# Modulation of mixer 0 loaded in four pieces of columns, gate sums moved into the products and chunks

## What is computed

```python
mod = (silu(c) @ ada_w + ada_b)                       # 6 * 1024 columns
sh1, sc1, g1, sh2, sc2, g2 = split(mod, 6)
h = rmsnorm(x, norm1_g) * (1 + sc1) + sh1
x = x + g1 * hybrid_mixer(h, ...)                     # w_in, conv, SSD chunks, gMLP, w_out
h = rmsnorm(x, norm2_g) * (1 + sc2) + sh2
x = x + g2 * conv_gated_ffn(h, ...)
out = rmsnorm(x, final_g)
```

## Time and profile before

| | |
|---|---|
| median of 3 runs | 2769.61 us (2765.91 to 2772.1) |
| profiled execution, its own time | 2763.87 us |
| its span | 2762.1 us |
| TensorE busy in the span | 2697.5 us |
| VectorE, ScalarE, GpSimd busy | 1815.1, 1003.4, 1072.4 us |
| granted TensorE clock, mean of the span | 0.994 |

### The profile page before, as it was taken

The page is one execution under the profiler, slowest core; times in us unless marked ns, Lnnn a source line. Parts: engine busy times, 40 slices in busy tenths (PEclk is TensorE's granted clock), DMA queues, the critical chain, the costliest instruction groups (busy, mean ns, idle before and its releaser), DMA issues.

```text
span 2762.1 us, 33801 instructions
## 1 busy us (share of the span) xinstructions
PE 2697.5 (98%) x12427; PEld 2207.2 (80%) x12427; DVE 1815.1 (66%) x2544; ACT 1003.4 (36%) x1521; POOL 1072.4 (39%) x739
## 2 busy tenths in 40 slices
PE   7999999999999999999999999999999999999998
PEld 6777887787878888887878888888888788887886
DVE  6977956768287565568787565555746855455767
ACT  3543325321153333343535322152223433334333
POOL 3444435445057777654650100001102544444240
PEclk9999999999999999999999999999999999999999
DMA  9876877999846566483448767587676334445646
GB/s 383 281 268 246 313 263 248 349 328 315 287 129 218 201 207 217 157 293 96 148 160 298 236 211 280 177 284 235 210 261 201 117 116 127 126 125 207 217 167 221
DMA packets 261872, 616.29 MB, mean 223 GB/s; under 512 B 26597, under 2 KB 84425, under 8 KB 257611
## 3 DMA queue, kind: packets, MB, share of 16 engines
q1 hardware_dynamic: 261046, 613.89, 64.9%
q10 hardware_dynamic: 662, 0.24, 0.0%
HBM read 462.37 MB, written 151.66 MB: 222 GB/s over the span
## 4 chain that ended last, share of the span: by engine, by line
PE 82%; DVE 6%; DMA 5%; issue 3%; POOL 2%; SPq 1%; ACT 1%; DVEq 0%; ACTq 0%; POOLq 0%
PE main L2038 34%; PE pair L2310 15%; PE main L2310 14%; PE pair L2330 6%; PE main L2330 5%; DMA w_split_scratch<-w_hl 2%; PE pair L2179 2%; POOL w_hl L739 1%; PE pair L2204 1%; PE pair L2164 1%; PE pair L2171 1%; DVE a_lo L1659 1%; DMA ada_t<-in_ada_w_dram 1%; DMA w_hl<-w_split_scratch 1%; POOL tb L750 1%
## 5 line engine op out<-in xcount | busy, mean ns | idle before, releaser
L739 POOL TENSOR_TENSOR w_hl<-w_raw,w_hl 128x512 fp32r<-128x512 f32 x548 | 794.2, 1455 | 920.5 <-ACT w_hl L844 918.8
L844 ACT ACTIVATE w_hl<-w_raw 128x512 fp32r<-128x512 f32 x548 | 342.3, 630 | 831.9 <-PE main L2310 169.4
L2038 PE MATMUL main<-w_hl,h_hi 128*128 128x512 f32 x1536 | 493.4, 403 | 5.1 <-DMA w_hl<-w_split_scratch 2.8
L2038 PEld LDWEIGHTS main<-w_hl,h_hi 128*128 128x128 f32 x1536 | 285.9, 189 | 77.8 <-issue 14.7
L2038 PE MATMUL main<-w_hl,h_lo 128*128 128x512 f32 x768 | 301.3, 392 | 0.0
L781 POOL TENSOR_TENSOR pre_hl<-pre_raw,pre_hl 128x512 fp32r<-128x512 f32 x35 | 51.0, 1461 | 566.3 <-ACT pre_hl L868 566.3
L2038 PE MATMUL main<-h_hi,w_hl 128*128 128x512 f32 x768 | 247.7, 396 | 7.4 <-POOL w_hl L739 4.2
L750 POOL TENSOR_TENSOR tb<-tb,tb 128x512 f32<-128x512 f32 x132 | 198.1, 1501 | 113.9 <-DMA tb<-in_ff_up_dram 109.5
L2310 PE MATMUL pair<-s_hi,w_hl 128*128 128x512 f32 x736 | 235.8, 393 | 2.4 <-POOL w_hl L739 2.4
L2330 PE MATMUL main<-w_hl,a_hi 128*128 128x512 f32 x704 | 219.2, 393 | 7.3 <-DVE a_lo L1659 3.9
L1659 DVE TENSOR_TENSOR a_lo<-g,a_hi 128x512 fp32r<-128x512 f32 x132 | 160.8, 1226 | 96.6 <-ACT a_hi L1094 96.1
(11 more groups left out here) (297 smaller groups left out, 5055.3 us busy)
## 6 DMA issues: line engine op xcount, KB each, us to landing
w_hl<-w_split_scratch SPq DMA_DIRECT2D x296, 512.0 KB, 4.4
w_split_scratch<-w_hl SPq DMA_DIRECT2D x104, 512.0 KB, 7.1
w_raw<-t_up_scratch SPq DMA_DIRECT2D x176, 256.0 KB, 2.7
w_raw<-in_ff_up_dram SPq DMA_DIRECT2D x132, 256.0 KB, 3.6
w_raw<-in_w_in_dram SPq DMA_DIRECT2D x88, 256.0 KB, 6.1
tb<-in_ff_up_dram SPq DMA_DIRECT2D x88, 256.0 KB, 5.0
t_up_scratch<-tb SPq DMA_DIRECT2D x88, 256.0 KB, 4.1
g_scratch<-c_val SPq DMA_DIRECT2D x44, 512.0 KB, 4.0
```

Source lines behind the costliest of these rows:

```text
L739: nc.gpsimd.tensor_tensor(w_lo[:, g % RING, :], w_raw[:, g % RING, :], w_hi[:, g % RING, :].bitcast(F32), ALU.subtract).then_inc(w_lo_ok, 1)
L844: nc.scalar.activation(w_hi[:, g % RING, :], w_raw[:, g % RING, :], ACT.Copy).then_inc(w_hi_ok, 1)
L2038: ins = T.matmul(main[i], a, w, start=first and p == 0, stop=last and p == 2)
```

## The change

The first third of ada_w is loaded as four **pieces** p of 256 columns of sh1 and the same 256 of sc1, each as two halves of four row slices (4 DMAs of 512 KB, in rows of 1 KB). Units 0 to 7 are loaded between the pieces. Of pieces 0 and 1 TensorE takes the first four row slices directly (`DIRECT`); VectorE sums the rest by `piece_sum` in steps of 128x512: 4, 4, 8 and 8. Each piece is turned into columns after unit 0, 2 or 4 (piece 0 before unit 0) and gives two tiles of h. The transposes use three banks; x is scaled by ScalarE and VectorE, two tiles each; each tile of x has a semaphore of its own. The gate tiles are loaded at units 8 to 27 and summed where `gate_sum` stands; the gate products move from unit 23 to chunk 1, give four rows of one bank with a `pick` matrix, and one addition over four rows takes the place of four. Column loads 0, 1 and 2 move from units 28, 20 and 40 to 31, 41 and 43, the gates' bias from 20 to 29, the store of the gates from 30 to 42, the spatial weights ws from the start to unit 12.

```diff
+        PIECES, HF0, ADA_SEMS, DIRECT = 4, 4, 12, (4, 4, 0, 0)
+        PW = D // PIECES
+        PIECE_SUMS = [sum(KD - d for d in DIRECT[:p + 1]) for p in range(PIECES)]
...
-        GATE_TILES = {8: 12, 11: 13, 14: 14, 17: 15}
-        COL_AT = {20: 1, 28: 0, 40: 2, 48: 3, 56: 4, 68: 5, 78: 6, 84: 7}
-        GATES_SUMMED = 2 * KD - ADA_PE
+        GATE_AT = {8: 0, 10: 1, 13: 2, 15: 3, 18: 4, 21: 5, 24: 6, 27: 7}
+        COL_AT = {31: 0, 41: 1, 43: 2, 48: 3, 56: 4, 68: 5, 78: 6, 84: 7}
...
+            def piece_load(p, half):
+                rows_h = ada_w[0, 4 * half * P:(4 * half + 4) * P, :].rearrange("(k p) (s d) -> p k s d", p=P, d=D)
+                for part in range(2):
+                    sp.dma_start(ada_p[p][:, 4 * half:4 * half + 4, part, :], rows_h[:, :, part, p * PW:(p + 1) * PW]
+                                 ).then_inc(ada_in[2 * p + half], 16)
+
+            def gate_load(g):
+                if g >= 4:
+                    sp.wait_ge(mod_col, PIECES)
+                if g == 7:
+                    sp.wait_ge(ada_summed, GATES_FROM + 3)
+                src = ada_w[0, g * P:(g + 1) * P, :].rearrange("p (h m d) -> p h m d", h=2, m=3)[:, :, 2, :]
+                sp.dma_start(ada_g[g].rearrange("p (m d) -> p m d", m=2), src).then_inc(ada_in[g], 16)
...
-                sp.dma_start(xn01[:, t, :] if t < 2 else xn23[:, t - 2, :], x[0, t * P:(t + 1) * P, :]).then_inc(x_in, 16)
...
-                ada_load(i)
-            for n in range(RING):
-                xbc_unit(0, n)
+                sp.dma_start(xn01[:, t, :] if t < 2 else xn23[:, t - 2, :], x[0, t * P:(t + 1) * P, :]).then_inc(ada_in[8 + t], 16)
+            piece_load(0, 0)
+            piece_load(0, 1)
+            xbc_unit(0, 0)
+            xbc_unit(0, 1)
+            piece_load(1, 0)
+            piece_load(1, 1)
+            xbc_unit(0, 2)
+            xbc_unit(0, 3)
+            xbc_unit(0, 4)
+            piece_load(2, 0)
+            xbc_unit(0, 5)
+            piece_load(2, 1)
...
-            for i in range(KD, ADA_RING):
-                ada_load(i)
-            for i in range(ADA_RING, 2 * KD):
-                xbc_unit(0, i - ADA_RING + RING)
-            sp.dma_start(ws_raw[:], gm_ws[0].rearrange("h t s -> t h s")).then_inc(pro_dma, 16)
+            piece_load(3, 0)
+            xbc_unit(0, 6)
+            piece_load(3, 1)
+            xbc_unit(0, 7)
...
-                    sp.wait_ge(gate_mm, 4)
+                    sp.wait_ge(ada_summed, GATES_FROM + 4)
                 elif k == 1:
-                    sp.wait_ge(ada_summed, KD + 3 - ADA_PE)
+                    sp.wait_ge(gate_mm, 1)
+                elif k == 2:
+                    sp.wait_ge(ada_summed, GATES_SUMMED + 1)
...
-                    sp.wait_ge(ada_summed, GATES_SUMMED + k)
+                    sp.wait_ge(ada_summed, GATES_SUMMED + (2 if k == 3 else k))
...
-                if b == 0 and n in GATE_TILES:
-                    ada_load(GATE_TILES[n])
+                if b == 0 and n in GATE_AT:
+                    gate_load(GATE_AT[n])
                 if b == 0 and n in COL_AT:
                     col_load(COL_AT[n])
-                if b == 0 and n == 20:
-                    sp.wait_ge(mod_col, 3)
+                if b == 0 and n == 12:
+                    sp.dma_start(ws_raw[:], gm_ws[0].rearrange("h t s -> t h s")).then_inc(pro_dma, 16)
+                if b == 0 and n == 29:
+                    sp.wait_ge(ws_ok, 2)
                     for g in range(2):
-                        sp.dma_start(gate_rows[0:1, g * D:(g + 1) * D], ada_b[:, (2 + 3 * g) * D:(3 + 3 * g) * D]
-                                     ).then_inc(bias_in, 16)
-                if b == 0 and n == 30:
-                    sp.wait_ge(gate_ok, 4)
-                    sp.dma_start(gate_d.rearrange("g d -> (g d)").unsqueeze(0), gate_rows[0:1, :]).then_inc(gate_stored, 16)
+                        sp.dma_start(gate_rows[2 * g:2 * g + 2, :], ada_b[0, (2 + 3 * g) * D:(3 + 3 * g) * D].rearrange(
+                            "(h n) -> h n", n=W)).then_inc(bias_in, 16)
...
+            h_low0(3)
+            low(RING + 1)
+            low(RING + 2)
+            h_low0(4)
+            h_low0(5)
+            for n in range(RING + 3, MU):
                 low(n)
             first_step = RAW_TO - 4
             for n in range(RAW_FROM, RAW_TO):
...
-            for t in range(NT):
-                tile = xn01[:, t, :] if t < 2 else xn23[:, t - 2, :]
+            for t in range(2):
+                tile = xn01[:, t, :]
...
-                act.wait_ge(ready, 1 + k // 4)
-                h_tiles(0, (k,), C_SC1, C_SH1, aux)
+                act.wait_ge(ready, 1 + k // 2)
+                h_tiles(0, (k,), C_SC1, C_SH1, aux[0:3])
                 if 2 <= k < 2 + HF0:
-                    act.wait_ge(h_lo_ok, 2)
-                    nc.scalar.activation(acc[:, k % 2, :], aux[k % 4], ACT.Identity, bias=mod_c[:, C_SH1 + k:C_SH1 + k + 1],
+                    act.wait_ge(h_lo_ok, max(2, k - 1))
...
-                if k >= 4:
-                    split(k)
+                for n in {1: (4,), 3: (5, 6), 5: (7,)}.get(k, ()):
+                    split(n)
...
-                if t == 0:
-                    dve.wait_ge(x_in, 16 * NT * (p + 1))
+                if p == 0:
+                    dve.wait_ge(ada_in[8 + t], 16)
+                elif t == 0:
+                    dve.wait_ge(x_in, 16 * NT * p)
...
+            def piece_sum(p, k):
+                dve.wait_ge(ada_in[2 * p + k // 4], 32)
+                weighted(mod_sum[:, 0:2, p * PW:(p + 1) * PW], ada_p[p][:, k, :, :], k, k == DIRECT[p])
...
+            def gate_sum(g):
+                dve.wait_ge(ada_in[g], 48)
+                weighted(flat(2), ada_g[g][:], g, g == 0)
...
+            dve.wait_ge(xr_ok, 1)
+            for t in range(2):
+                V.tensor_scalar(xn23[:, t, :], xn23[:, t, :], rstd[:, t + 2:t + 3], None, ALU.mult).then_inc(xn_ok, 1)
...
+            for p in range(PIECES):
+                for k in range(DIRECT[p], KD):
+                    piece_sum(p, k)
+                ks = slice(2 * p, 2 * p + 2)
+                base = two_parts(col_b, R_AB, ks)
+                if p == 0:
+                    dve.wait_ge(col_ok, 2)
+                if DIRECT[p]:
+                    dve.wait_ge(mod_col, p + 1)
+                    link(V.tensor_tensor(two_parts(mod_c, 0, ks), two_parts(aux[3] if p else main[1], 0, ks), base, ALU.add))
+                    base = two_parts(mod_c, 0, ks)
+                mod_columns(0, ks, aux[3][:, 2 * KD:] if p else main[3], base, R_N1, p + 1)
+                if p == 0:
+                    dve.sem_inc(evacuated, 4)
+                    h_lows(0, (0, 1), aux[0:3], full_at)
+            dve.wait_ge(h_lo_ok, KD - 2)
+            h_lows(0, (KD - 2, KD - 1), aux[0:3], full_at)
...
+                    gate_sum(0)
 
...
-                        ada_sum(KD + 4)
+                        gate_sum(1)
...
-                        ada_sum(KD + 5)
-                        ada_sum(KD + 6)
+                        gate_sum(2)
+                        gate_sum(3)
...
-                        for m in range(4):
-                            dve.wait_ge(gate_mm, m + 1)
-                            row = gate_rows[0:1, m * W:(m + 1) * W]
-                            V.tensor_tensor(row, aux[m][0:1, :], row, ALU.add).then_inc(gate_ok, 1)
+                    if b == 0 and j == 2:
+                        gate_sum(5)
                     if b and j == 0:
                         scan()
...
+                    if b == 0 and cc < NT - 1:
+                        if cc == 0:
+                            gate_sum(6)
+                        else:
+                            col_sum(2 * cc - 2)
...
+                    if b == 0 and cc == 1:
+                        dve.wait_ge(bias_in, 32)
+                        dve.wait_ge(gate_mm, 1)
+                        V.tensor_tensor(gate_rows[:], aux[3][0:4, :], gate_rows[:], ALU.add).then_inc(gate_ok, 1)
...
-                        col_sum(cc + 1)
+                            gate_sum(7)
+                        else:
+                            col_sum(2 * cc - 1)
 
...
+            def mod_direct(p, bank):
+                pe.wait_ge(ada_in[2 * p], 32)
+                for part in range(2):
+                    for kt in range(2):
+                        m = part * KD + 2 * p + kt
+                        for k in range(DIRECT[p]):
+                            T.matmul(bank[:, m:m + 1], ada_p[p][:, k, part, kt * P:(kt + 1) * P], c_act[:, k:k + 1],
+                                     start=k == 0, stop=k == DIRECT[p] - 1)
+
+            def piece_column(p, bank):
+                pe.wait_ge(ada_summed, PIECE_SUMS[p])
+                mod_column((2 * p, 2 * p + 1), bank)
...
-            mod_direct(main[1], range(KD))
+            mod_direct(0, main[1])
...
-            h_transpose(0, range(4), xn, aux)
+            h_transpose(0, range(3), xn, aux[0:3])
...
```

(28 more changed lines are left out.)

121 lines of the change are left out of this document (42 added, 79 removed).

## The result

The changed kernel took a median of 2773.19 us (20 runs, 2768.05 to 2778.14), the kernel before, beside it, 2766.60 us (20 runs, 2759.62 to 2772.41): ratio 1.0024, interval 1.0016 to 1.0031, or 4.4 to 8.6 us **slower**. The forecast was 2769.5 us and no change. The time lies inside the range of 2761.5 to 2776.5 us, but the sign isn't the one forecast. Ratios compare executions of the fast state; one execution of the kernel before, in the second series of the experiments, took 6998.51 us and is left out of them.

A forecast was written before the change was run, and what follows sets the result against it. TensorE, busy 2697.5 of 2762.1 us, was taken to bound the kernel. An earlier start of 4.2 us less 2.8 and 1.3 given back left 0.1 won: 2769.5 us, no change, range 2761.5 to 2776.5.

The forecast's parts named there:

- G: Start: how much earlier unit 8 begins; 6.8 us undisturbed, 4.2 taken, between 0.5 and 6.8.
- Price of a one-column product: Start, TensorE: 0.22 us for each direct or column product, from 3.58 / 16.
- The sums of pieces 2 and 3: Start, VectorE: eight sums cost 5.8 us a piece; 3.5 steps lengthened by GpSimd cost 3.6 less 1.0 slack, 2.6.
- The low clock between the pieces: Start, TensorE: each gap that lowers the clock costs a unit 1.5 to 1.9 us, 6 to 7 for four pieces.
- rival C: Start: seven long sums or low clock between pieces make longer gaps; total 3.6 to 6 us slower; chance 0.12.
- three signs of being wrong: Unit 8 before 57 or after 65 us; low clock after 31; TensorE's waits from 150 to 260 growing over 3 us.
- Landings: Start, DMA queue: a MiB in rows of 1 KB lands in 2.9 us, between 2.54 and 3.4.
- Chunks: Mixer 0, chunks 0 and 1: 2.8 us given back, and 1.3 for a new wait in chunk 1.
- The wait for the decayed x: Chunk 0: TensorE waits 1.3 to 3.4 us, middle 2.3, for the state product's input.
- Edits at nothing: Moved sums, loads, stores and SP's stands at units 41 and 42 cost nothing; SP's 6.2 us at unit 28 goes.
- rival D: Chunks 1 to 3: SP's stands and 3 MiB more make stores land later; 7 us slower, 5 to 9; chance 0.16.
- Rival B: Start and chunk 0: TensorE, not VectorE, sets the pace; 8 to 10 us faster; chance 0.18.

The follow-up runs named there:

- the two second traces: The kernel before and the changed kernel, both unaltered, each traced once more; the changed one had unit 0 at 30.64 and unit 8 at 68.15 us.
- late_direct: Changed kernel with the 16 direct products of piece 1 moved from ahead of unit 0 to behind it; 2779.59 us, ratio 1.0050.
- few_lows: Changed kernel with low parts of units 4 to 7 and low halves of tiles 2 to 5 made for 8 columns, GpSimd nearly idle; 2771.57 us.
- gate4_late: Changed kernel with gate tiles 4 and 5 loaded at units 20 and 22 instead of 18 and 21; 2773.64 us, ratio 1.0023.
- sum6_behind: Changed kernel with only gate sum 6 moved behind the decayed x of chunk 0; run once for its trace, 2769.79 us.
- gates_behind: Changed kernel with gate sum 6 behind the decayed x, gate products behind the state-to-output product, and column loads 1, 2 and gate store later; 2770.40 us.
- sp_later: Changed kernel with column loads 1 and 2 and the gate store at units 43, 45 and 44; run once for its trace, 2767.71 us.
- direct4: Changed kernel with the first four row slices of pieces 2 and 3 also as direct products on TensorE; 2774.23 us, ratio 1.0028.

## Why the prediction was wrong, step by step

**The forecast's sum** was G = +4.2, -2.8, -1.3: 0.1 won. Measured up to unit 40: -4.2, then -1.3, then -4.2. The failed step is **G**, how much earlier unit 8 starts: +4.2 forecast, -4.2 measured (-2.0 between the two second traces), and in it above all the price of a one-column product, 0.22 us forecast and 0.44 measured.

1. *Price of a one-column product.* The forecast took 0.22 us, from "one-column products took 3.58 / 16". The 16 were records; the product is two of them, 0.44 us. The kernel before shows it in its own rows; each of these three groups is 16 products in the code:

```profile
15.04 6.96 PE L2005 MATMUL main<-c_act,ada_t 128*128 128x1 f32 x32 [12.26 <-DMA ada_t<-in_ada_w_dram]
...
25.80 3.77 PE L2005 MATMUL main<-c_act,ada_t 128*128 128x1 f32 x32
32.17 6.98 PE L1995 MATMUL main<-tri,mod_sum 128*128 128x1 f32 x32 [2.61 <-DVE mod_sum L1252]
```

   So 0.44 us at the low clock, 0.23 at the high one: the 0.22 would have been about right at the high level, at which neither group ran in the changed kernel's traces. Twice 16 products in the new start cost 13.6 us instead of 7. The first group's 3.3 us more made the columns of piece 0 late (25.4 instead of 21.5), the second group, which at 0.22 us each would have ended well ahead of the first product, ended as unit 0 began. First product: 26.6 forecast, 31.27 measured (28.4 and 27.9 in two traces, where the group took 4.2 and 4.5); second part of the columns at 38.2 instead of 33.7: **4.5 us**. late_direct shows which of these dates counts: not unit 0's, but the columns', because VectorE's sums of piece 2 stand behind them in its order.
2. *The sums of pieces 2 and 3.* 5.8 forecast for eight, 9.0 measured. The first takes 0.59 us and a further one 0.86 with its gap, not 0.35 and 0.78 (+0.7), and three steps are hit in each run, not 3.5 in both together (+2.5). Columns of piece 2 at 49.1 instead of 42.0, of piece 3 at 59.7 instead of 50.3: **2.6 and 2.3 us** more. few_lows shows it by removal. The forecast had seven candidates and took half, by a count over all work to 137 us of one long step for two GpSimd operations; in these two stretches VectorE does nothing but two-input steps behind a first one, six operations stood beside them and six steps were long. The lower end of G was that case.
3. *The low clock between the pieces*, in rival C at 1.5 to 1.9 us a gap, came in units 3 and 5 after the waits of 2.2 and 1.8 us: **1.4 us** behind piece 3 (unit 5 took 4.4 us), the one behind piece 2 hidden by VectorE's next run. The 1.4 is what is left when the others are taken off; no run isolates it.

4.5 + 2.6 + 2.3 + 1.4 = 10.8 us is the way from the undisturbed 58.2 to 69.0. The forecast had allowed 2.6 of them, for the long steps; the other 8.2, and 0.2 between 65.0 and 64.83 as the old start of unit 8, are the 8.4 by which G is off. Nearest to the kernel is rival C, "the change doesn't do what it says", with a chance of 0.12: its long steps and its low clock both came. But it hasn't the largest term, the 4.5 us, so G went beyond its -2, and that its total of 2773.2 to 2775.6 us stands beside a time of 2773.19 is luck. Of the three signs of being wrong two came, unit 8 after 65 us and a low granted clock after 31; the third, TensorE's waits from 150 to 260 us, stayed just under its 3 us (2.7 before, 5.5 after).

**What held.** *Landings:* taken at 2.9 us a MiB for rows of 1 KB, between 2.54 and 3.4; the 2 MiB of piece 1 landed between unit 1, at 17.3 us, and 23.4, 3.0 a MiB. VectorE waited for no piece behind piece 0. *Chunks:* -2.8 and -1.3, 4.1 us given back; measured 4.2 (5.2) from unit 23 to 40. The wait for the decayed x was forecast at 1.3 to 3.4, middle 2.3: 1.8, 2.9 and 2.4, but 0.5 in gate4_late. The gate products 3.6: 3.60. The wait for the gate rows 1.3: 1.5. sum6_behind and gates_behind show by removal that gate sum 6 and the place of the gate products cost 3.8 of the 4.2. The close sum owes something to luck: unit 24 gains 4.0 us where 3.1 was forecast, and of the 8.2 lost from there to unit 40 the three terms are 6.9; the other 1.3 wasn't forecast and isn't located. *Edits at nothing:* SP's stands at units 41 and 42 cost nothing (sp_later) and stores landed no later, so rival D falls; SP's 6.2 us at unit 28 did go. *Rival B* falls: VectorE did set the pace, and with direct4, where it doesn't, TensorE is slower still.

**What was left out.** "Through unit 17 the queue carries 4 MiB less", so nothing was charged there; but the load of gate tile 4 moved to unit 18, ahead of the store on which a split waits, and ScalarE's copies stand behind that split: 2.5 us at unit 16 (gate4_late), of which 1.3 is left at unit 23, no more than two traces of one kernel differ there. Bytes in sum don't tell it; the order of one load and one store does.

**What stays open.** The three causes at unit 40 are 9.7 us against a first trace of before that was 2.7 us under its median; by its second trace 7.3. Which 0.8 to 3 us of these the runs don't see (4.4 to 8.6) lies in what moves between executions behind unit 40 and isn't shown by any run. For the same reason a gain at unit 40 isn't a gain in time one for one: direct4 and few_lows differ there by 5.7 and 3.8 us from the changed kernel, and by 1.0 and 1.6 us in their medians. Why late_direct is 6 us over the changed kernel, and not 2.4, is open too.

## What to carry to other kernels

Count instructions in the code and records in the trace before dividing one by the other; a price off by two in a group that stands first on its engine moved everything behind it here. When a load is cut into pieces, write down VectorE's list for each piece: the piece's columns, not the first product, are the date that counts, and sums of a later piece belong into the wait for an earlier one's columns (7 us here, with the same bytes). A sum or a load moved out of the start is not free where it lands: ask which product waits for the step behind it, and which store stands behind it in the queue.
